# Two edits to a two-block kernel: the order of the first weight loads, and what stands directly behind TensorE's branch

## What is computed

```python
for l in range(2):                       # first block
    h = rms_norm(x, attn_norm[l])
    proj = h @ w_in[l]                   # 1024 x 2568, used in six column groups
    hm, ha, hc = mlstm(proj, m_conv_w, ...), mla(proj, a_w_uq, a_w_ukv, ...), gating(proj, c_w_s, ...)
    x = x + head_norms(hm, ha, hc) @ w_out[l]
    x = x + hier_moe(rms_norm(x, ffn_norm[l]), ...)   # 32 experts, top 2 in one group of 8
x = second_block(x, w_in_2, ...)         # starts with rms_norm(x) @ w_in_2
```

## Time and profile before

| what | value |
|---|---|
| runs of the kernel | 1127.41, 1123.24, 1126.16 us |
| median | 1126.16 us |
| the profiled execution | 1124.19 us, with a span of 1122.0 us |
| mean granted clock of TensorE | 0.986 of full speed |
| TensorE busy | 1064.3 us (95% of the span) |
| VectorE, ScalarE, GpSimd busy | 405.3, 267.7, 101.9 us |
| HBM read | 288.03 MB |

### The profile page before, as it was taken

How to read it: one execution, slowest core, us unless ns; L and a number is a source line. 1 busy time by engine, 2 the same in 40 slices (tenths; PEclk the granted TensorE clock), 3 DMA queues, 4 the chain that set the end, 5 groups by cost and what they waited for, 6 DMA issues and landing times.

```text
span 1122.0 us, 12894 instructions
## 1 busy us (share of the span) xinstructions
PE 1064.3 (95%) x4555; PEld 543.5 (48%) x4589; DVE 405.3 (36%) x985; ACT 267.7 (24%) x509; POOL 101.9 (9%) x148
## 2 busy tenths in 40 slices
PE   6999989999999988999989999999999999999898
PEld 4676644333333334676544333333335744555443
DVE  2362344444333531372353443443531212333220
ACT  3435321111111114235311111111020015454300
POOL 1320121000000002210130000000000200000000
PEclk9999999999999998999999999999999999989999
DMA  8528208999999996027219999999979249421000
GB/s 301 184 76 300 76 38 328 412 413 412 412 412 411 413 380 198 1 103 273 76 43 384 412 411 412 413 412 412 413 277 389 86 49 310 183 85 65 0 1 38
DMA packets 95596, 280.79 MB, mean 250 GB/s; under 512 B 16136, under 2 KB 29878, under 8 KB 87232
## 3 DMA queue, kind: packets, MB, share of 16 engines
q1 hardware_dynamic: 90192, 273.27, 64.0%
q0 software_dynamic: 5360, 6.94, 1.8%
HBM read 288.03 MB, written 4.72 MB: 261 GB/s over the span
## 4 chain that ended last, share of the span: by engine, by line
PE 67%; SPq 23%; DMA 3%; issue 2%; ACT 2%; DVE 2%; ACTq 0%; DVEq 0%
SPq L556 15%; PE bank L1421 13%; PE bank L892 9%; PE bank L1001 7%; PE bank L1195 5%; PE bank L1015 5%; PE bank L924 4%; SPq L562 4%; PE bank L845 3%; SPq L603 3%; PE bank L1563 2%; PE bank L1547 2%; PE bank L1438 2%; PE bank L834 2%; DMA ring<-in_w 1%
## 5 line engine op out<-in xcount | busy, mean ns | idle before, releaser
L892 PE MATMUL bank<-ring,arena 128*64 128x512 f32 x1024 | 229.6, 596 | 9.6 <-DMA ring<-in_w 9.4
L1421 PE MATMUL bank<-ring,xfT 128*128 128x512 f32 x320 | 144.5, 608 | 0.0
L892 PEld LDWEIGHTS bank<-ring,arena 128*64 128x64 f32 x1024 | 72.6, 137 | 142.0 <-issue 130.5
L924 PE MATMUL bank<-ring,arena 128*64 128x512 f32 x512 | 116.9, 598 | 0.0
L1001 PE MATMUL bank<-ring,xfT 128*128 128x384 f32 (+2 forms) x256 | 98.6, 540 | 3.5 <-DMA ring<-in_w_in 3.5
L1421 PEld LDWEIGHTS bank<-ring,xfT 128*128 128x128 f32 x320 | 61.1, 194 | 76.1 <-issue 76.1
L845 PE MATMUL bank<-arena 128*128 128x512 bf16 x352 | 86.4, 379 | 1.9 <-issue 0.3
L1909 DVE TENSOR_TENSOR arena<-bank,arena 128x512 f32<-128x512 f32 x60 | 41.5, 692 | 119.4 <-ACT arena L1585 119.4
L1585 ACT ACTIVATE arena<-bank 128x512 bf16<-128x512 f32 (+1 forms) x64 | 38.3, 598 | 190.0 <-PE bank L924 190.0
L1001 PEld LDWEIGHTS bank<-ring,xfT 128*128 128x128 f32 x256 | 49.5, 198 | 44.7 <-issue 30.7
L1578 ACT ACTIVATE arena<-bank,arena 128x256 f32<-128x256 f32 x32 | 15.2, 476 | 218.7 <-PE bank L892 218.7
(11 more groups left out here) (374 smaller groups left out, 1118.5 us busy)
## 6 DMA issues: line engine op xcount, KB each, us to landing
ring<-in_w SPq DMA_DIRECT2D x256, 512.0 KB, 14.9
ring<-in_w SPq DMA_DIRECT2D x64, 1024.0 KB, 14.0
ring<-in_w_in SPq DMA_DIRECT2D x14, 2048.0 KB, 19.7
ring<-in_w_in SPq DMA_DIRECT2D x8, 1536.0 KB, 17.4
ring<-in_w_out SPq DMA_DIRECT2D x6, 2048.0 KB, 7.6
ring<-in_w_in SPq DMA_DIRECT2D x2, 1696.0 KB
x_store<-x POOLq DMA_DIRECT2D x4, 512.0 KB, 3.0
ring<-in_w_up_moba SPq DMA_DIRECT2D x1, 2048.0 KB
```

What stands on the lines that cost most here:

```text
L892: ins = pe.matmul(bank[5][CELL * e:CELL * (e + 1), :], xg[:, par, 4 * h + k, at:at + CELL], view[:, e, :, k, :], start=(h == 0 and k == 0) ...
L924: ins = pe.matmul(bank[5 + n][CELL * e:CELL * (e + 1), :], turned[:, par, c, CELL * e:CELL * (e + 1)], down_view(s)[:, e, c, n * HALF:(n + ...
L1421: ins = pe.matmul(dst[:, :], xfT[:, k, t * P:(t + 1) * P], w[:, k, :], start=(k == 0), stop=(k == KD - 1))
```

## The change

It has two parts.

1. Unit 2 of layer 0 is loaded in two halves of four k's each. The first half is issued ahead of x's tile 1 and raises a semaphore of its own, `loaded_half`; the second is issued behind x's tile 1 and raises `landed[2]`. The loop over the units skips unit 2 in layer 0, and `mixer_loads(0)` moves from between units 2 and 3 to between units 3 and 4. TensorE waits for the first half ahead of k 0 of `b1t0`, for the second ahead of k 4.
2. TensorE's branch is turned round. The case without overflowing cells stands directly behind it and holds `turn(l + 1)`; the overflow code is the other case and ends with a `turn(l + 1)` too. The loop's own `turn` is left for layer 0 alone, and `turn(DEPTH)` ahead of the second block is gone, since layer 1's branch makes it.

```diff
             sp.dma_start(gain_cols[:, DEPTH, :], io["norm_w_2"]).then_inc(loaded_first, 16)
-            sp.dma_start(x[:, 1, :], io["x"][0, P:2 * P, :]).then_inc(loaded_x[1], 16)
+            for half in range(2):
+                c0, c1 = UNIT_COLS[2]
+                sp.dma_start(unit_view(2, c1 - c0)[:, 4 * half:4 * half + 4, :],
+                             io["w_in"][0, half * HALF:(half + 1) * HALF, c0:c1].rearrange("(k p) n -> p k n", p=P))\
+                  .then_inc(loaded_half if half == 0 else landed[2], 16)
+                if half == 0:
+                    sp.dma_start(x[:, 1, :], io["x"][0, P:2 * P, :]).then_inc(loaded_x[1], 16)
...
                     for s in UNIT_ORDER:
-                        if l == 0 and s == UNIT_ORDER[1]:
+                        if l == 0 and s == UNIT_ORDER[2]:
                             mixer_loads(l)
                         c0, c1 = UNIT_COLS[s]
-
+                        if l == 0 and s == UNIT_ORDER[0]:
+                            continue
                         sp.wait_ge(freed[s], l * layer_uses[s] + 1)
...
                     if k0 == 0:
                         dst = open_bank(name)
-                        lands(u, 1)
                     else:
                         dst = bank[plan[name][0]]
+                    if l == 0 and name == "b1t0" and k0 == 0:
+                        pe.wait_ge(loaded_half, 16)
+                    elif k0 == 0 or name == "b1t0":
+                        lands(u, 1)
...
             for l in range(DEPTH):
-                turn(l)
+                if l == 0:
+                    turn(0)
                 mix(l)
...
                 close_banks(l)
-                with pe.If(n_over > 0):
+                with pe.If(n_over < 1):
+                    turn(l + 1)
+                with pe.Else():
                     S = extra[l]
...
                     last_combine(extra_sums[l])
-                with pe.Else():
-                    pe.nop()
+                    turn(l + 1)
...
             if second:
-                turn(DEPTH)
                 last_block()
```

More of the change, by code:

```diff
@@ L378, in program @@
         loaded_first = sem("loaded_first")
+        loaded_half = sem("loaded_half")
         loaded_positions = sem("loaded_positions")
```

## The result

The changed kernel takes 1133.76 us (median of 6 runs, 1131.64 to 1137.47) against 1126.36 us for the kernel before (6 runs beside it): ratio 1.0071, 95% interval 1.0055 to 1.0086. It is slower by 0.7%, 7.4 us. I had forecast 1125.8 and no difference.

The account below looks back on a forecast made before the run. TensorE-bound stretches alternate with stretches bound by SP's loads. 1124.19 - 0.9 (start) + 0 (layer 0's end) + 1.5 (layer 1's end) = 1124.8 against the profile, 1126.8 against the median; middle 1125.8, range 1121.5 to 1130 us.

Parts of the forecast that it names:

- the start gains 0.9 us: Start of layer 0: the unit after the small transposes starts at 26.7 instead of 27.55; bounds 2.1 gained, 1.7 lost.
- the 4.0 us for the 1471 KB of small loads: Start: time for layer 0's mixer loads behind slot 3 and POOL's constants, at the pace of slots 3 and 4.
- the queue does not run dry: Start: small loads are issued while slot 3 flows, so their landing was taken as 25.0, nearer the byte sum.
- handed on: Start: SP waits for ring slots TensorE frees, so the start's gain or loss passes to both in later stages.
- small loads last: Rival, start: mixer loads land at slot 3's old time, next unit at 29.2, 1.7 us later; total 1127.4; chance 0.14.
- The end of layer 0: Between layers: removing most of the 3.09 us pause gains 0, since the 4.32 us wait for w_ukv takes it in.
- The end of layer 1: Ahead of the last block: the jump moves behind the turns, block starts at 839.1 instead of 837.60, 1.5 us lost.
- 2.5 to 3.0: End of layer 1: cost in us of the jump behind the turns, with only half a microsecond of turns beside it.
- my bound of 3.7: End of layer 1: largest loss in us, if the jump behind the turns takes 5.0.
- The clock: Rival, last block: a 3.7 us bare jump, then seven slow records, 2.4 us; together 6.1, to 1130.3; chance 0.08.
- Two terms that I had called extremes: Whole kernel: only two terms' extremes together leave the 0.5% band; faster 0.03, slower 0.05, same 0.92.
- My own sign of being wrong: Start: a wait above 3 us at the small transposes (L1072) would show the forecast wrong; about 1.4 us was expected.

Follow-up runs that it names:

- e4: Kernel before with only layer 0's small loads moved behind unit 3, unit 2 as one load: 1127.58 us, ratio 1.0014.
- e6: Kernel before without the branch, its value_load and the overflow code on TensorE: 1124.75 us, ratio 0.9990.
- e1: Changed kernel with TensorE's branch and turns as before, so only the load changes remain: 1128.71 us, ratio 1.0027 to the kernel before.
- e7: Changed kernel with SP holding back the second block's loads after the first unit until x's squares are done: 1130.27 us, ratio 1.0035 to the kernel before.
- e2: Kernel before with only the branch turned round and the turns in its short case, loads as before: 1131.83 us, ratio 1.0050.

## Why the prediction was wrong

Two steps failed: the price of the small loads at the start, and the price of the jump at the end of layer 1. Behind both stood the slow clock, which the sum left out.

**The start, step by step.** x's second tile at 9.3 (9.5 measured), first products at 11.2 (11.34), no wait for the second half (none), arrival at the small transposes at 23.6 (23.4): right, the last in part by luck, since e4 arrives at 23.4 too with unit 2 loaded as before. The landing of the small loads was taken as 25.0, between 23.8 and 27.54; it was 26.69, and there "the start gains 0.9 us" broke. The term that failed is the 4.0 us for the 1471 KB of small loads, priced at the pace of the large ones, with the premise that the queue does not run dry. They took 7.9 us behind unit 3, at a DMA share that fell to 0.58; unit 3 itself came at 18.8, about 1 us ahead of the sum's 19.8. I also left out that a wait slows what follows it, 2.7 us. In place of 0.9 gained, 3.5 were lost in this stage; at the end of layer 1 1.7 of them were left, so "handed on" held only in part.

I had set aside the rule of the Trainium skill (DMA: Bandwidth & Descriptors, Queues, rings and completion order), by which a small load waits on each engine for unit 3's part, because it seemed to put the landing at the late end. That was misread: 27.54 is where unit 3 landed behind the small loads, and ahead of them it landed at 18.8. The rule does not account for the 26.69. The rival "small loads last" had the next unit at 29.2 and it began at 29.52, but by another sum than the rival's: the loads did not land with unit 3.

**The end of layer 0** was put at 0, and the wait for `w_ukv` did take the pause in. e6 shows it from the other side, where 9.54 us of wait take in all that is gained. But I expected the wait for `w_ukv` to grow; it shrank to 1.53, since a pause of 4.50 had come ahead of it. From the last product of layer 0 (418.72, 4.3 us later than before) to the end of the next unit's products (2.3 later) the changed kernel even made up 2 us. In e1, with the branch as before, it is 1 us, so how much of this the branch has a part in is not shown.

**The end of layer 1.** The mechanism was forecast as it came: the jump is not removed but put behind the turns, a pause ahead of the last block, a packet in it. The term "2.5 to 3.0" for the jump was too small. I had taken the time from the packet's start to the first instruction behind it, and that part held (841.04 to 843.85, 2.8). What I left out is the time that passes before the packet begins, 2.4 us from the end of the last turn (the trace does not show the jump itself). Before, this part lay beside the last product and could not be seen. In e7, with idle DMA engines, the packet comes before the turns have ended. Measured: 4.6 us where I had 1.5; my bound of 3.7 was too low too.

**The clock** ahead of the last block was a rival to which I gave 0.08, at 2.4 us; it cost 2.4 us (27.70 to 30.09), behind a pause of 5.20. That the price came out is partly luck: no row stood behind the count of seven slow records.

**The band.** Two terms that I had called extremes, and the clock, came together. They were not independent: both parts of the change made a pause on TensorE, 3.32 and 5.20 us, and behind each the granted clock fell to 0.50. My own sign of being wrong, a wait above 3 us at L1072, had come true. With 0.92 on no difference I had left no room for it. e1 and e2 each lie within 0.5% of before or on its edge; only their sum leaves it.

The buffer of 2048 instructions that the Trainium skill (Runtime: NRT & Kernel Launch, Instruction fetch mechanics) gives TensorE did not make this jump free, in either kernel; how many instructions the jump passes over, no row shows. The same section says that a taken branch whose target is outside the fetched window forces a fetch. The traces agree: a 16 KB instruction packet stands 2.5 to 3.0 us ahead of the first instruction behind each pause (418.7 and 832.6 before, 426.8 and 841.0 after, 424.5 and 837.5 in e7), and e6 has none in that queue (q8) from 415 to 424 nor from 827 to 840.

## What to carry to other kernels

A jump like this one, with nothing queued on TensorE behind it, left a pause of about 5 us while the DMA engines were busy (4.5 to 5.5 in five places here), and of 2.9 while they were idle; taken beside the last product it left 0.5 to 3.1 (0.54 and 1.79 in e1, 1.06 and 3.09 before). So leave it where products are still in flight, not behind a wait. Before loads are reordered, split the semaphore: what the first user needs goes first, and large weights that hide among "small" loads go behind. Do not price many small loads at the pace of large ones: 1471 KB in 16 loads took 7.9 us where the byte count gave 4.0. And price a pause with the slow clock that follows it, not by its length alone.

## What I had not expected of the hardware

The instruction packet of a jump is held up by data transfers. With DMA's share at 1.06 in the windows, 2.4 us passed between the last turn and the packet; with a share of 0.00 the packet began before the last turn had ended, and the pause fell from 5.20 to 2.85 us. The kernel before points the same way without meaning to. Its two packets stand 2.5 us apart against the end of the last product, 0.6 behind it and 1.9 ahead of it, and the traffic ahead of them differed, in its windows:

```profile
416.00:418.70 2.70, 2.15 (x6) 0.60 (x4) 2.05 (x3) 0.00 (x0) 0.00 (x0) 1.00 1.04 366
830.50:832.60 2.10, 2.10 (x6) 0.81 (x5) 0.00 (x0) 0.60 (x1) 0.00 (x0) 1.00 0.67 246
```

It is not the only thing that moves the packet: in e1 the first of the two begins at 420.3, 0.8 us ahead of the last product's end, with a share of 1.04 in the 2.3 us before it.
